# A two-layer hybrid decoder step on one core: the rotary swap as small SBUF-to-SBUF transfers, and one score matrix counted by ScalarE

## The reference

```
def partial_rope(x, cos, sin):            # ROT_DIM = 16 of 64 columns of a head
    x1, x2 = x[..., :8], x[..., 8:16]
    return concatenate([x1 * c - x2 * s, x2 * c + x1 * s, x[..., 16:]], axis=-1)

def indexer_scores(qi, wi, ki, valid):
    dots = einsum('bqhd,bsd->bqsh', qi, ki) * 64 ** -0.5
    sc = einsum('bqsh,bqh->bqs', relu(dots), wi) * 8 ** -0.5
    return where(valid, sc, -inf)
# then _, sel = top_k(sc, topk), and softmax attention over the selected keys
```

## Time and profile before

| | us |
|---|---|
| median of 3 runs | 2644.62 |
| lowest and highest | 2642.03, 2655.07 |
| span of the profiled execution | 2645.1 |

### The profile page before, as it was taken

One profiled execution on the slowest core, in us unless ns is written; L12 is line 12 of the kernel. 1 busy time (PEld: TensorE's weight loads), 2 busy tenths in 40 slices (PEclk: granted clock), 3 DMA queues, 4 the chain that ended last, 5 costly groups with the idle time before them and its releaser, 6 DMA issues.

```text
span 2645.1 us, 51365 instructions
## 1 busy us (share of the span) xinstructions
PE 2503.9 (95%) x20020; PEld 2304.4 (87%) x20020; DVE 1797.7 (68%) x3095; ACT 1127.1 (43%) x2070; POOL 1286.0 (49%) x973
## 2 busy tenths in 40 slices
PE   5979999999998999999999989999889999999999
PEld 4847864677898999999999989999889999999998
DVE  6388988665248666656667687767695665656775
ACT  5155656775135444444212363332454444442223
POOL 2403652443135656556544535545355656555444
PEclk8999999999899999999999999999999999999999
DMA  9205557202334444344985233328324434369731
GB/s 321 78 22 160 174 206 254 63 2 81 114 102 113 139 130 162 122 152 143 342 328 183 97 97 106 106 90 328 100 85 150 155 117 161 126 210 364 288 131 70
DMA packets 316388, 407.98 MB, mean 154 GB/s; under 512 B 40816, under 2 KB 227032, under 8 KB 313338
## 3 DMA queue, kind: packets, MB, share of 16 engines
q1 hardware_dynamic: 316154, 404.75, 45.7%
HBM read 284.85 MB, written 119.85 MB: 153 GB/s over the span
## 4 chain that ended last, share of the span: by engine, by line
PE 65%; DVE 15%; DMA 6%; issue 5%; POOL 4%; ACT 3%; SPq 2%; DVEq 0%; ACTq 0%; POOLq 0%
PE PS L589 9%; PE PS L2456 9%; PE PS L2458 9%; PE PS L2457 9%; PE PS L2500 5%; PE PS L2502 5%; PE PS L2503 5%; PE PS L1835 3%; PE PS L1864 2%; PE PS L1846 2%; DMA t_scratch<-stage 2%; POOL ring L2775 2%; DMA a_scratch<-stage 1%; DVE s_all L1532 1%; POOL stage L2788 1%
## 5 line engine op out<-in xcount | busy, mean ns | idle before, releaser
L2456 PE MATMUL PS<-th,ring 128*128 128x264 f32 x2800 | 802.7, 287 | 28.0 <-DVE y L2920 9.4
L2458 PE MATMUL PS<-th,ring 128*128 128x264 f32 x2800 | 798.7, 285 | 0.0
L2457 PE MATMUL PS<-th,ring 128*128 128x264 f32 x2800 | 797.9, 285 | 0.0
L2456 PEld LDWEIGHTS PS<-th,ring 128*128 128x128 f32 x2800 | 529.9, 189 | 35.4 <-issue 30.3
L2457 PEld LDWEIGHTS PS<-th,ring 128*128 128x128 f32 x2800 | 530.1, 189 | 0.0
L2458 PEld LDWEIGHTS PS<-th,ring 128*128 128x128 f32 x2800 | 530.1, 189 | 0.0
L2775 POOL TENSOR_TENSOR ring<-wraw,ring 128x512 fp32r<-128x512 f32 x232 | 339.5, 1468 | 359.9 <-ACT ring L2579 359.3
L2775 POOL TENSOR_TENSOR ring<-sums,ring 128x512 fp32r<-128x512 f32 x216 | 319.9, 1483 | 284.0 <-ACT ring L2579 283.8
L2500 PE MATMUL PS<-th,ring 128*128 128x264 f32 x1232 | 352.4, 286 | 13.6 <-DVE zs L3089 6.4
L2502 PE MATMUL PS<-th,ring 128*128 128x264 f32 x1232 | 351.2, 285 | 0.0
L2503 PE MATMUL PS<-th,ring 128*128 128x264 f32 x1232 | 350.7, 285 | 0.0
(11 more groups left out here) (371 smaller groups left out, 5187.4 us busy)
## 6 DMA issues: line engine op xcount, KB each, us to landing
t_scratch<-stage SPq DMA_DIRECT2D x154, 528.0 KB, 3.4
th<-t_scratch SPq DMA_DIRECT2D x77, 1056.0 KB, 8.8
wraw<-in_ffn_w_gu_dram SPq DMA_DIRECT2D x96, 512.0 KB, 5.2
wraw<-in_ada_w_dram SPq DMA_DIRECT2D x80, 512.0 KB, 4.9
wraw<-in_ffn_w_down_dram SPq DMA_DIRECT2D x80, 256.0 KB, 6.0
wraw<-in_conv_w_in_dram SPq DMA_DIRECT2D x28, 512.0 KB, 5.2
y<-y_scratch SPq DMA_DIRECT2D x12, 1056.0 KB, 8.7
y_scratch<-y SPq DMA_DIRECT2D x6, 2112.0 KB, 8.2
```

Of the source, the lines that this page charges most:

```text
L2456: pe.matmul(out, hi, x[:, TH, k, :], start=(k == 0 and i in (1, 2, 5)), stop=False, skip_group_check=True)
L2457: pe.matmul(out, hi, x[:, TL, k, :], start=False, stop=False, skip_group_check=True)
L2458: last = pe.matmul(out, lo, x[:, TH, k, :], start=False, stop=(k == 3), skip_group_check=True)
```

## The change

It has two parts.

**The rotary swap.** The 45 products with `rotm`, its constant and its load go, and ScalarE's 30 copies `act_rot` too. ScalarE issues instead, right after its own evacuation of a tile, two (r < 3) or four DMAs of 8 partitions by 352 columns each, from `psgA` to `pafA` or from `psgB` to `pafB` (`act_swap`): 54 in the first projections and 120 in the later ones. The rows that are never written are zeroed once, by VectorE at the start and by GpSimd ahead of the later projections. Whoever used the product waits for the two semaphores `swapped`, and in the first projections VectorE's multiplication reads SBUF instead of PSUM. The next evacuation into the same buffer waits for the swap that reads it.

**The search.** `NA` becomes 3: the samples' matrix goes into the first group, and ScalarE counts it right behind the 896 count. The list `COUNT_AT` stays. VectorE waits for three counts before its comparison, counts four matrices, and makes the four closing steps for three.

```diff
-        def pe_rot(pe, r):
-            rows = P if r >= 3 else 64
-            pe.wait_ge(evac, rope_m(r) + 1)
-            after(pe, ts_rdy, r - 1)
-            src = (psgA if r < 15 else psgB)[0:rows, r % 2, :]
-            pe.matmul(rot_bank(r)[0:rows, 0:CH], rotm[0:rows, 0:rows], src, start=True, stop=True).then_inc(rot_mm, 1)
+        def swap_done(eng, r):
+
+            if r >= 0:
+                eng.wait_ge(swapped[r % 2], sum(32 if x < 3 else 64 for x in range(r % 2, r + 1, 2)))
+
+        def act_swap(act, r):
+
+            act.wait_ge(evac, rope_m(r) + 1)
+            after(act, fin_rdy, r - 1)
+            if r in (15, 16):
+                act.wait_ge(pm_rdy, 1)
+            src, dst = (psgA, pafA) if r < 15 else (psgB, pafB)
+            for head in (0,) if r < 3 else (0, 64):
+                for o in (head, head + 8):
+                    of = 2 * head + 8 - o
+                    act.dma_start(dst[o:o + 8, r % 2, :], src[of:of + 8, r % 2, :]).then_inc(swapped[r % 2], 16)
...
+                    if j:
+                        act.activation(junkC[0:NS, :], s_smp[0:NS, :], ACT.Sign, bias=bv[0:NS, CAND + 2:CAND + 3],
+                                       scale=-1.0, accum_out=bv[0:NS, BS + 2:BS + 3]).then_inc(sign_cnt, 1)
...
         def act_evac_rope(act, p, n, dst):
             m, r = m_at(p, n), R_AT[p] + n
             rows = P if p else 72
             act.wait_ge(up_mm, UP_END[p] - 2 + n)
-            after(act, rot_mm, r - 1)
+            swap_done(act, r - 2)
...
         def act_proj_a(act):
             for p in range(5):
                 for n in range(NCH):
                     if p or n:
                         act_evac_rope(act, p, n, psgA)
+                    act_swap(act, 3 * p + n)
                 proj_hi(act, p + WR)
...
                 for n in range(NCH):
                     act_evac_rope(act, p, n, psgB)
                     act_count(act, 2 * (ITEM_AT[p] + n))
-                    act_rot(act, R_AT[p] + n - 1)
+                    act_swap(act, R_AT[p] + n)
                     if n == 0 and p <= 13:
                         proj_hi(act, p + 3)
...
-            dve.wait_ge(rot_mm, r + 1)
-            after(dve, fin_rdy, r - 1)
-            dve.tensor_tensor(pafA[0:rows, r % 2, :], rot_bank(r)[0:rows, 0:CH], ropeS[0:rows, chunk(n)], ALU.mult)\
+            if r == 0:
+                dve.wait_ge(const_loaded, 48)
+            swap_done(dve, r)
+            dve.tensor_tensor(pafA[0:rows, r % 2, :], pafA[0:rows, r % 2, :], ropeS[0:rows, chunk(n)], ALU.mult)\
                 .then_inc(ts_rdy, 1)
...
-        NA = 2
+        NA = 3
...
                 small(2, 0, i)
-                count(NA + 3, None)
+                signal(count(NA + 3, None))
                 dve.wait_ge(sel, i * 7 + (base + 2))
                 small(3, 0, i)
-                signal(count(NA + 4, None))
-                dve.wait_ge(sel, i * 7 + (base + 4))
+                dve.wait_ge(sel, i * 7 + (base + 3))
                 small(1, 1, i)
...
-            entries = [tile(7), tile(6), tile(2), tile(5), tile(4), tile(3), (s_smp[0:NS, :], NS, LS, KS)]
+            entries = [tile(7), tile(6), (s_smp[0:NS, :], NS, LS, KS), tile(2), tile(5), tile(4), tile(3)]
```

More of the change, by code:

```diff
@@ L492, in program @@
         f_sq, f_st, f_af, f_hi, f_lop, f_lod, f_smp = (sem(f"f_{x}") for x in ("sq", "st", "af", "hi", "lop", "lod", "smp"))
-        evac, rot_mm, ts_rdy, pm_rdy, qc_rdy, fin_rdy = (sem(x) for x in (
-            "evac", "rot_mm", "ts_rdy", "pm_rdy", "qc_rdy", "fin_rdy"))
+        evac, ts_rdy, pm_rdy, qc_rdy, fin_rdy = (sem(x) for x in ("evac", "ts_rdy", "pm_rdy", "qc_rdy", "fin_rdy"))
+        swapped = [sem(f"swapped{i}") for i in range(2)]
         q_stored = [sem(f"q_stored{i}") for i in range(3)]
@@ L675, in dve_start @@
             dve.memset(ones[:], 1.0)
+            dve.memset(pafA[:], 0.0)
             dve.memset(bv[:, 0:9], 1.0).then_inc(f_st, 1)
@@ L924, in pe_proj_a @@
         def pe_proj_a(pe):
-            pe.wait_ge(const_loaded, 64)
+            pe.wait_ge(const_loaded, 48)
             pe.wait_ge(ada_read, G0)
@@ L943, in pe_proj_a @@
             last.then_inc(kiw_mm, 1)
-            pe_rot(pe, 14)
         def pe_turn_k(pe, tt):
@@ L1000, in act_evac_rope @@
                            scale=-SC if ORDER[p] < 8 else 1.0).then_inc(evac, 1)
[L1002 to L1006, removed]
         def act_proj_a(act):
@@ L1105, in pool_fin @@
             p, n = (5, r - 15) if r < 18 else (8 + (r - 18) // 3, r % 3)
-            pool.wait_ge(ts_rdy, r + 1)
+            swap_done(pool, r)
             pool.tensor_tensor(pafB[:, r % 2, :], pafB[:, r % 2, :], ropeS[:, chunk(n)], ALU.mult).then_inc(pm_rdy, 1)
-            pool.wait_ge(pm_rdy, r - 14)
+            pool.wait_ge(pm_rdy, r - 13)
             pool.wait_ge(qc_rdy, r + 1)
@@ L1121, in pool_proj_b @@
         def pool_proj_b(pool):
+            pool.wait_ge(relu_rdy, 8 * len(TILES))
+            pool.wait_ge(qs_rdy, 2)
+            pool.memset(pafB[:], 0.0).then_inc(pm_rdy, 1)
             for p in (5,) + tuple(range(8, 17)):
@@ L1543, in junk @@
         def junk(j, rows, L):
-            at = (0, 1024, None, 1920, 2688, 3328, None)[j]
+            at = (0, 1024, None, None, 1920, 2688, 3328)[j]
             if at is None:
-                return junkB[0:rows, :] if j == 2 else junkC[0:rows, :]
+                return junkB[0:rows, :] if j == 3 else junkC[0:rows, :]
             return junkA[0:rows, at:at + L]
@@ L1653, in dve_select @@
                 s, rows, L, k = entries[j]
-                A = relu[:, j, 0:L]
-                link(dve, dve.tensor_scalar(A, s, one(th, j), -NEG, ALU.is_le, ALU.mult))
+                A = relu[0:rows, j % 2, 0:L]
+                link(dve, dve.tensor_scalar(A, s, one(th, j)[0:rows], -NEG, ALU.is_le, ALU.mult))
                 link(dve, dve.tensor_tensor(A, A, s, ALU.max))
-                link(dve, dve.tensor_reduce(one(cand, j), A, AX_X, ALU.min))
-                link(dve, dve.tensor_scalar(A, s, one(cand, j), 0.0, ALU.is_ge, ALU.add, accum_out=one(cnt, j)))
+                link(dve, dve.tensor_reduce(one(cand, j)[0:rows], A, AX_X, ALU.min))
+                link(dve, dve.tensor_scalar(A, s, one(cand, j)[0:rows], 0.0, ALU.is_ge, ALU.add, accum_out=one(cnt, j)[0:rows]))
             link(dve, dve.tensor_tensor(v(ge, 0, NA), v(cnt, 0, NA), v(kk, 0, NA), ALU.is_ge))
@@ L1667, in dve_mask_step @@
             s, rows, L, k = entries[j]
-            out = mask_s[0:rows, :] if j == 6 else mask_of((7, 6, 2, 5, 4, 3)[j])
+            out = mask_s[0:rows, :] if j == 2 else mask_of((7, 6, None, 2, 5, 4, 3)[j])
             A, B = mscr[0:rows, 0, 0:L], mscr[0:rows, 1, 0:L]
@@ L3455, in _constants @@
     cos, sin = np.cos(ang).T, np.sin(ang).T
-    C, S, R = np.ones((P, T), np.float32), np.zeros((P, T), np.float32), np.zeros((P, P), np.float32)
+    C, S = np.ones((P, T), np.float32), np.zeros((P, T), np.float32)
     for o in (0, 64):
@@ L3459, in _constants @@
         S[o:o + 8], S[o + 8:o + 16] = -sin, sin
-        for d in range(8):
-            R[o + 8 + d, o + d] = R[o + d, o + 8 + d] = 1.0
     q, x = np.arange(P)[:, None], np.arange(SEQ)[None, :] - (SEQ - P)
```

29 lines of the change are left out of this document (5 added, 24 removed).

## The result

The changed kernel takes 2658.97 us (median of 8 runs, 2649.52 to 2663.91), before takes 2649.99 in the same comparison (8 runs, 2642.03 to 2655.07): ratio 1.0039, 95% interval 1.0025 to 1.0052. So it is slower by 0.4%, some 10 us: within the 0.5% of "no change" and just inside the range (2660), but on the other side of before than the forecast of 2638.5, and the interval leaves out 1. Its profiled execution has a span of 2660.0 against 2645.1.

The account below looks back on a forecast made before the run. Bounds: TensorE in first projections, VectorE in the index stage, the ScalarE-VectorE exchange in later projections. Terms -5.25 - 1.3 + 2.0 - 1.5 = -6.05 gave 2639.0 for the profiled execution, 2638.5 for the median; range 2629 to 2660.

Parts of the forecast that it names:

- The first projections: Stage from 60 to 128 us: -7.95 + 1.5 + 1.2 = -5.25, passed on whole by the index stage.
- The 7.95 of products: First projections: rotary products leaving TensorE's path before tile 14 ends, 7.95 together.
- the wait for cached keys: First projections: TensorE reaches the cached index keys' transposition before they land; 1.5 taken, bounds 0.9 and 4.
- the last swap: End of first projections: evacuation, issues, landing, product and addition take 5.7 after the last tile, so +1.2.
- The issue: Swap DMAs on ScalarE's queue: 0.43 each, up to 0.70, 1.72 per item, hidden beside the counts.
- The first twelve rounds: Search, 12 rounds taking 64.4, 5.37 each; four end without an evacuation in the chain: 2.2 off.
- the chain of 5.26: Search: one round of data passed between ScalarE and VectorE, third count included, sums to 5.26.
- The seventeen rounds after them: Search, later 17 rounds: 5.33 each falls to 5.26, 17 x 0.07 = 1.2 off.
- The end of the search: Third item and last two with counts: swap between two counts costs 0.55 each, 1.6 in all.
- The closing steps: After the last count: samples' count saves 0.77, closing a third matrix costs 2.8; together +2.0.
- The start of attention: TensorE some 10 us ahead, so query reload and conditioning weights start earlier: -1.5, bounds 0 and -4.
- The fast rival: Later projections: TensorE sets the pace and all 30 products count, 17.7: about 2622, chance 10%.

Follow-up runs that it names:

- e1: Changed kernel with the search of before (NA back to 2, VectorE counts the samples' matrix), swap by transfers kept: 2646.39 us, ratio 0.9990 to before.
- e9: e1 with weight split and key copy ahead of the issues, in items 34 and 35 issues behind both counts, memset in two pieces: 2644.28 us, 0.9982.
- e11: e9 with the zeroing of the landing area moved to GpSimd ahead of its first work: 2645.62 us, ratio 0.9985 to before.
- e3: Changed kernel with 36 unread TensorE products behind the last projection tile and 16 behind the first scores: 2659.50 us, ratio 1.0042 to before.
- e5: Changed kernel once more, unaltered, run and profiled a second time: 2655.97 us, ratio 1.0030 to before.
- e8: e7 with 30 unread TensorE products of 512 columns behind the last projection tile: 2648.82 us, ratio 0.9995 to before.
- e7: e1 with VectorE's one small memset at the start split into four: 2647.91 us, ratio 1.0000 to before.

## Why the prediction went the wrong way

**The first projections** were put at -5.25. They gave -0.6 in the profiled execution, -3.5 in the second profile of the kernel, -3.7 in e1. The 7.95 of products did leave the path. Against it stood, in the profiled execution: the wait for cached keys 2.27 and one of 0.47 (1.5 taken), two tiles in 9.22 instead of 7.7, since the clock fell behind that wait (0.69 in the stretch below, 1.00 there in before), and the last swap at +3.2 instead of +1.2. Together -7.95 + 2.27 + 0.47 + 1.5 + 3.2 = -0.5, near the -0.6 measured.

```profile
96.00:101.00 5.00, 3.85 (x17) 3.85 (x18) 0.67 (x2) 1.41 (x2) 2.36 (x2) 0.69 0.87 244
```

Two of the terms were mis-sized. The issue was priced at SyncE's 0.43; on ScalarE it is 0.63. (The prediction also took 0.70 for SyncE's longest single issue; the trace of before has one of 7.28 at 48.57, beside a median of 0.37.) And the rope's product was taken at 0.52 without a hold-up, while the last one took 2.7, about the length of GpSimd's part of the weight split beside it. That part waits for ScalarE's split, which stood behind the issues until 123.72:

```profile
124.86 2.71 DVE L1075 TENSOR_TENSOR pafA<-pafA,ropeS 128x352 f32<-128x352 f32 x1 [3.79 <-DMA pafA<-psgA]
```
```profile
124.86 2.34 POOL L827 TENSOR_TENSOR ulo<-wraw,uhi 128x1024 fp32r<-128x1024 f32 x1 [2.88 <-ACT uhi L821]
```

The same product at 119.92, with GpSimd idle, took 0.53. The rule of the Trainium skill ("SBUF — State Buffer", Reading the diagram) that the prediction weighed there, that a VectorE instruction with two SBUF inputs and a GpSimd instruction that reads SBUF exclude each other, was the better guide: the trace agrees with it (2.71 beside 2.34, 0.53 alone).

**The first twelve rounds** of the search are the step of the prediction that failed: 2.2 was taken off, because the chain of 5.26 was compared with a mean of 5.37. That mean hides what a list of the rounds shows. Eight of the twelve took 4.97 or 4.98, the pace of VectorE's five counts, and one took 7.30, a stall. The chain with the third count is 5.26, as summed, and so longer than those rounds, not shorter. They took 64.42 before and 67.51 after, +3.1. The chain was right and was compared with the wrong number. With the next two items the search came out at +7.7 instead of -1.3, which is most of the miss.

**The seventeen rounds after them** were put at -1.2 and gave +1.0 (90.66 and 91.70). Rounds of 5.39 fell to 5.27, as forecast; those of 5.17 to 5.23 rose to it, and some rose further (5.92, 5.59, 5.86), because splits and key copies wait behind 2.6 of issues. The forecast was right that the issues run beside the counts, but they end 3.1 after the evacuation's start (337.64 to 340.73) and not 2.2, and it gave no price to the splits and key copies behind them.
**The end of the search** holds two of the three items priced at 0.55 each, and was mis-sized. From the 1024 count at 356.49 (357.85 now) to the end of the counts it took 12.76 before and takes 16.36: +0.1 and +1.5 in two rounds and +1.95 behind the last 1024 count. The issues between two counts leave ScalarE idle for 1.48 each time, and a third count of 0.7 follows the last one. **The closing steps** held: +2.0 forecast, +2.15 and +3.2 in the two profiles. **The start of attention** was put at -1.5, and no gain came. From the first minimum to the last product with the values the changed kernel took 269.6 and, in the second profile, 265.3; before took 265.4. The last evacuations now wait for issues, and with them the query stores and the weight load queued behind these on SyncE (issued at 377.94, before at 373.67). TensorE idled 9.3 for that load (372.75 to 382.04), and its clock fell. The forecast named 8 to 10 us of idle time and gave it no price.

**The fast rival** (TensorE sets the pace) was out for the changed kernel, where the chain is longest. In e1, without the third count, VectorE sets it, with 5.12.

What the two halves do together is the heart of it. Taking the products off TensorE lets its rounds of 5.2 to 5.4 fall to VectorE's 5.12. Taking the samples' count off VectorE would let that fall as well, but puts it into the exchange, which then needs 5.27. So the second half relieved VectorE by lengthening the chain that runs through both engines, beyond what VectorE alone had needed.

## What to carry to other kernels

Where two engines hand a result to and fro, moving work from one to the other can lengthen the round: sum the chain once round, and compare it with the rounds one by one, not with their mean. The DMAs that ScalarE issued cost nothing for the work ahead of them in the program and held up the work behind them, so put issues behind whatever others wait for; what that gains, look for at the next thing that waits, for 4.6 in the search of e9 were 2.4 at the start of attention, and none in e11. Price an issue on the queue that will carry it, and when a transfer's landing is on the path count issue, landing and the reading instruction with whatever it may have to share.

## What the runs showed of the hardware

- An issue of 8 partitions by 352 columns from ScalarE took 0.63 (median of the 174 in the changed kernel, the longest 1.23; 2.61 to 2.65 for four), where the median of SyncE's 853 issues of other shapes is 0.38. The last one of the first projections landed 1.85 after its start.
- A VectorE product of 128x352 with both inputs in SBUF took 0.53 alone and 2.71 beside a GpSimd subtraction that started in the same moment and took 2.34.
- VectorE's search loop turned with a wait of 0.26 instead of 0.12 in every kernel with transfers for the swap, in both forms of the search; neither form, nor none to three more instructions ahead of the loop, changed it. Open.
- From its first relu copy to the first count of the search the program took one of two lengths, near 68.4 or near 70.5, with no difference in the instructions of the index stage between the kernels. Open as well.
- After TensorE's idle time of 9.3 the granted clock stayed at 0.50 for the first 27 us of attention in one execution of the changed kernel, and had a mean of 0.66 over the first 20 us and 1.00 after that in another. With the idle time filled the mean granted clock of the timed runs was 0.977 instead of 0.976 (e3 and e5, e8 and e7), and no gain showed in the medians.
